# Ranking the experts of a mixture on chip, with 32 token places for 44 of them

## The reference

```python
s = jax.nn.sigmoid((t @ router_w).astype(jnp.float32))
choice = s + router_bias.astype(jnp.float32)
...
_, eidx = lax.top_k(jnp.where(emask, choice, -jnp.inf), TOP_K)
...
gates = jnp.sum(jax.nn.one_hot(eidx, N_EXPERTS, dtype=jnp.float32) * w[..., None], axis=1)

def expert_step(acc, p):
    wg, wu, wd, g = p
    hid = jax.nn.silu(t @ wg) * (t @ wu)
    return acc + (hid @ wd) * g[:, None].astype(t.dtype), None

routed, _ = lax.scan(expert_step, jnp.zeros_like(t), (exp_w_gate, exp_w_up, exp_w_down, gates.T))
shared = (jax.nn.silu(t @ sh_w_gate) * (t @ sh_w_up)) @ sh_w_down
return (routed + shared).reshape(bsz, seq, d)
```

## Time and profile before

| | us |
|---|---|
| median of three runs | 1352.79 |
| lowest and highest of them | 1348.95, 1353.19 |
| the profiled execution | 1356.98 |
| its span, from the first to the last instruction | 1355.2 |
| TensorE busy in it | 1303.0 |
| VectorE busy | 484.7 |
| ScalarE busy | 324.2 |
| GpSimd busy | 77.8 |

### The profile page before, as it was taken

How to read it: one execution, slowest core, us unless ns; L and a number is a source line. 1 busy time by engine, 2 the same in 40 slices (tenths; PEclk the granted TensorE clock), 3 DMA queues, 4 the chain that set the end, 5 groups by cost and what they waited for, 6 DMA issues and landing times.

```text
span 1355.2 us, 17876 instructions
## 1 busy us (share of the span) xinstructions
PE 1303.0 (96%) x6452; PEld 711.2 (52%) x6452; DVE 484.7 (36%) x1079; ACT 324.2 (24%) x789; POOL 77.8 (6%) x100
## 2 busy tenths in 40 slices
PE   7988999999999999999799999999999999999995
PEld 4764744454444444544488857445544444445442
DVE  2583623333222333332432326333332223333324
ACT  3562212222121222221123222122121122221211
POOL 1352100000000000000150000000000000000000
PEclk8988899999999999999899999999999999999998
DMA  8162459999999999999861234599999999999991
GB/s 336 59 249 93 179 206 415 418 418 416 418 411 415 420 419 418 418 416 415 284 213 63 91 126 186 221 416 417 420 418 416 410 418 418 418 418 416 417 416 59
DMA packets 75730, 447.29 MB, mean 330 GB/s; under 512 B 7452, under 2 KB 20184, under 8 KB 25511
## 3 DMA queue, kind: packets, MB, share of 16 engines
q1 hardware_dynamic: 72640, 439.25, 79.6%
q0 software_dynamic: 1904, 6.46, 1.3%
q10 hardware_dynamic: 1142, 1.01, 0.2%
HBM read 445.61 MB, written 1.05 MB: 330 GB/s over the span
## 4 chain that ended last, share of the span: by engine, by line
PE 92%; DVE 2%; issue 2%; DMA 2%; ACT 1%; ACTq 0%; POOL 0%; DVEq 0%; POOLq 0%
PE bank L933 33%; PE bank L955 17%; PE bank L907 10%; PE bank L1001 9%; PE bank L757 4%; PE bank L793 4%; PE bank L861 2%; PE bank L670 2%; PE bank L943 2%; PE bank L796 2%; DMA mixT<-in_l_conv_w 1%; PE bank L970 1%; PE bank L899 1%; PE bank L630 1%; DVE side L1340 1%
## 5 line engine op out<-in xcount | busy, mean ns | idle before, releaser
L933 PE MATMUL bank<-ring,big 128*64 128x512 f32 x2048 | 446.5, 594 | 0.2 <-issue 0.2
L933 PEld LDWEIGHTS bank<-ring,big 128*64 128x64 f32 x2048 | 146.0, 137 | 278.0 <-issue 278.0
L955 PE MATMUL bank<-ring,big 128*64 128x512 f32 x1024 | 233.9, 599 | 2.2 <-ACT big L1213 2.2
L1609 DVE SCALAR_TENSOR_TENSOR ys_low<-bank,gcol,ys_high 128x512 fp32r<-128x512 f32 x128 | 96.1, 751 | 204.1 <-ACT ys_high L1219 204.1
L1601 DVE TENSOR_TENSOR big<-big,bank 128x256 f32<-128x256 f32 x64 | 27.0, 422 | 373.6 <-ACT big L1209 373.6
L907 PE MATMUL bank<-pick,xs_high 128*128 128x256 f32 x512 | 136.3, 302 | 0.0
L1219 ACT ACTIVATE ys_high<-bank,gcol 128x512 fp32r<-128x512 f32 x128 | 88.0, 688 | 192.0 <-PE bank L955 192.0
L955 PEld LDWEIGHTS bank<-ring,big 128*64 128x64 f32 x1024 | 67.8, 136 | 120.6 <-issue 109.7
L907 PE MATMUL bank<-pick,xs_low 128*128 128x256 f32 x512 | 126.5, 282 | 0.0
L1209 ACT ACTIVATE big<-bank 128x256 f32<-128x256 f32 x64 | 24.5, 383 | 405.8 <-PE bank L933 405.8
L907 PEld LDWEIGHTS bank<-pick,xs_high 128*128 128x128 f32 x512 | 97.6, 191 | 26.0 <-issue 24.8
(11 more groups left out here) (236 smaller groups left out, 1108.6 us busy)
## 6 DMA issues: line engine op xcount, KB each, us to landing
ring<-in_l_exp_w_gate SPq DMA_DIRECT2D x128, 1024.0 KB, 9.3
ring<-in_l_exp_w_up SPq DMA_DIRECT2D x128, 1024.0 KB, 11.4
ring<-in_l_exp_w_down SPq DMA_DIRECT2D x128, 1024.0 KB, 15.3
ring<-in_l_w_in SPq DMA_DIRECT2D x12, 1024.0 KB, 12.3
ring<-in_l_w_out SPq DMA_DIRECT2D x8, 1024.0 KB, 6.0
ring<-in_l_w_in SPq DMA_DIRECT2D x4, 1440.0 KB, 15.8
par<-in_l_ln_g POOLq DMA_DIRECT2D x4, 512.0 KB, 7.0
par<-in_l_ln_b POOLq DMA_DIRECT2D x4, 512.0 KB, 7.8
```

Source lines behind the costliest of these rows:

```text
L933: ins = mm(ps[SLOTS * q:SLOTS * q + SLOTS, :], xg[:, c, SLOTS * j:SLOTS * j + SLOTS], both[:, c], start=(c == 0), stop=(c == C - 1))
L955: ins = mm(ps[SLOTS * q:SLOTS * q + SLOTS, :], hidT[pr][:, m, SLOTS * q:SLOTS * q + SLOTS], wt[:, m, HALF * h:HALF * h + HALF], start=(m = ...
L1609: ins = v.scalar_tensor_tensor(ys[1][:, pr, part], ps[:], gcol[:, pr:pr + 1], ys[0][:, pr, part], ALU.mult, ALU.subtract)
```

## The change

The experts are ranked by their number of tokens, on chip. Experts 0 to 7 (`NATURAL`) keep ranks 0 to 7; the other 56 follow by falling count. Ranks 0 to 19 (`NWIDE`) are worked on as before, in five groups of 64 places: one "first", three "wide" and one "turn" (`KINDS`). The other 44 experts get 32 places (`NSLOT`), in eleven "narrow" groups of four. A further round runs if an expert has more tokens than the places of its rank.

The ranking takes place in the first group. VectorE compares the counts (`ranks`) and makes a permutation `perm`; TensorE flips `routed` (the old `posm` and `gates` in one tile) and multiplies it by `perm` (`sort`); VectorE reads the tables back in the new order, with the expert numbers by rank in `order` (`ordered`). SyncE loads the four expert numbers of a group from `order` ahead of its refill. Five small GpSimd operations prepare constants for it.

A narrow group runs in three stages of four weight units each: the gates of four experts in four column tiles of 32 places, then their ups, then their downs. Its gathers have 128 columns instead of 256 and go two chunks to a bank (`pairs`), and its scatter has 8 matmuls instead of 16. SyncE refills its units by kind: four gates, four ups, four downs (`BY_KIND`).

```diff
+NSLOT = 32
+NATURAL = 8
+KINDS = (("first", 1), ("wide", 3), ("turn", 1), ("narrow", 11))
+BEGIN = {"first": 0, "wide": 1, "turn": 4, "narrow": 5}
+NWIDE = GE * BEGIN["narrow"]
...
-        u.loop(L, seq, NGRP, but=("gather",))
+        narrow = [("gT", 0), ("gate", 0), ("up", 1), ("hT", 1)] + [(("dn", h), 2 + h) for h in range(2)] + pair
+        narrow += [(("scatter", n), 6 + n % 2) for n in range(4)]
+        times = dict(KINDS)
+        u.loop((L, "first"), wide + [("rowsT", 6), ("sorted", 7)] + gather + scatter, times["first"])
+        u.loop((L, "wide"), wide + gather + scatter, times["wide"])
+        u.loop((L, "turn"), wide + pair + scatter, times["turn"])
+        u.loop((L, "narrow"), narrow, times["narrow"], but=("pair",))
...
+    if kind == "narrow":
+        return ("gate", "up", ("dn", 1))[w]
     return ("gu", j // 2) if w < 2 else ("dn", j // 2, 1)
...
+BY_KIND = [(j, w) for w in range(3) for j in range(GE)]
...
+                def refill(lp, experts):
+
+                    for j, w in BY_KIND if lp.kind == "narrow" else IN_ORDER:
+                        lp.read(sp, last_use_of_weights(lp.kind, j, w))
+                        sp.dma_start(loop_weights(L, j, w), expert_weights(L, experts[j], w))\
+                          .then_inc(S(f"unit_full{loop_unit(L, j, w)[0]}"), 16)
+
+                def in_place(at):
+
+                    return [sp.value_load(order[0:1, bass.ds(at + j, 1)], min_val=0, max_val=NE - 1) for j in range(GE)]
+
+                refill(ExpertLoop(L, "first", banks, S, bank, i=0), [GE + j for j in range(GE)])
+                sp.wait_ge(S("order"), L + 1)
...
+                lp = ExpertLoop(L, "narrow", banks, S, bank)
+                with sp.Fori(0, dict(KINDS)["narrow"] - 1) as i:
+                    lp.i = i
+                    refill(lp, in_place(lp.groups(GE, GE)))
...
+                def pairs(lp, cs):
+
+                    n = GE * NSLOT
+                    for c in cs:
+                        ps = lp.open(pe, ("pair", c))
+                        for s in range(2):
+                            for tb in range(TB):
+                                for k in range(2):
+                                    ins = mm(ps[:, n * s:n * s + n], xs[k][:, tb, P * (2 * c + s):P * (2 * c + s) + P],
+                                             pick[:, tb, 0:n], start=(tb + k == 0), stop=(tb + k == 2))
+                        lp.made(ins, ("pair", c))
+
+                def sort(lp):
+
+                    lp.moved(pe, "rowsT")
+                    pe.wait_ge(S("perm"), L + 1)
+                    ps = lp.open(pe, "sorted")
+                    for tb in range(TB):
+                        mm(ps[:, P * tb:P * tb + P], routedT[:, tb, :], perm, start=True, stop=True)
+                    mm(ps[0:1, 2 * P:2 * P + NE], expert[0:NE], perm[0:NE, 0:NE], start=True, stop=True)
+                    ins = mm(ps[0:1, 3 * P:3 * P + NE], rank[0:NE, 1:2], perm[0:NE, 0:NE], start=True, stop=True)
+                    lp.made(ins, "sorted")
...
+                    if lp.kind == "first":
+                        ps = lp.open(pe, "rowsT")
+                        for tb in range(TB):
+                            ins = flip(ps[:, P * tb:P * tb + P], routed[:, tb, :, :].rearrange("p a b -> p (a b)"), ident[:])
+                        lp.made(ins, "rowsT")
                     pe.wait_ge(lp.sem("pick"), lp.count(2, 2, 0))
...
+                    for w, key in enumerate(("gate", "up")):
+                        ps = lp.open(pe, key)
+                        for j in range(GE):
+                            weights_landed(lp, j, w)
+                        for c in range(C):
+                            for j in range(GE):
+                                r = slice(NSLOT * j, NSLOT * j + NSLOT)
+                                ins = mm(ps[r, 0:HID], xn[:, c, r], loop_weights(L, j, w)[:, c, :],
+                                         start=(c == 0), stop=(c == C - 1))
+                        lp.made(ins, key)
+
+                    if not last:
+                        pe.wait_ge(lp.sem("pick"), lp.count(2, 2, 1))
+                        pairs(lp, (0, 1))
...
+                    lp.moved(pe, "hT")
+                    for j in range(GE):
+                        weights_landed(lp, j, 2)
+                    for h in range(2):
+                        ps = lp.open(pe, ("dn", h))
+                        for m in range(2):
+                            for j in range(GE):
+                                r = slice(NSLOT * j, NSLOT * j + NSLOT)
+                                ins = mm(ps[r, :], hidT[0][:, m, r], loop_weights(L, j, 2)[:, m, HALF * h:HALF * h + HALF],
+                                         start=(m == 0), stop=(m == 1))
+                        lp.made(ins, ("dn", h))
...
-                v.memset(gates[:], 0.0)
-                v.memset(posm[:], FAR)
...
+                def ranks():
+
+                    v.memset(perm, 0.0)
+                    link(v.tensor_tensor_reduce(where_key.rearrange("p (a e) -> p a e", a=2),
...
+                    link(v.tensor_scalar(over_cap, rank_key, rank[:, 1:2], None, ALU.is_gt))
+                    link(v.tensor_reduce(rank[:, 0:1], over_cap, AX.X, ALU.add))
+                    for half_of in range(2):
+                        at = slice(NE * half_of, NE * half_of + NE)
+                        ins = v.tensor_scalar(perm[at, at], iota[at, :], rank[at, 0:1], None, ALU.is_equal)
+                    ins.then_inc(S("perm"), 1)
+
+                def ordered(lp):
+
+                    ps = lp.read(dve, "sorted")
...
+                    v.tensor_copy(in_turn[:, :, :, 0:NE], ps[:, 0:TB * P].rearrange("p (a k e) -> p a k e", a=TB, k=2))
+                    v.tensor_copy(order[0:1, :], ps[0:1, 2 * P:2 * P + NE]).then_inc(S("order"), 1)
```

More of the change, by code:

```diff
@@ L282, in run_groups, with last_use_of_weights @@
             group(lp)
[L283 to L289 removed]
+    lp.u = 0
+def last_use_of_weights(kind, j, w):
+    if kind == "narrow":
+        return ("gate", "up", ("dn", 1))[w]
     return ("gu", j // 2) if w < 2 else ("dn", j // 2, 1)
@@ L1008, in prog_tensor @@
                 pe.wait_ge(S("xs"), 2 * L + 2)
-                pe.wait_ge(lp.sem("pick"), 1)
+                pe.wait_ge(S(f"moe{L}_pick"), 1)
                 for c in range(C):
                     bank_made(gather(c, bank_open(pe, ("gather", L, c))), ("gather", L, c))
-                run_groups(pe, lp, group)
+                wide(ExpertLoop(L, "first", banks, S, bank, i=0))
+                for i in range(dict(KINDS)["wide"]):
+                    wide(ExpertLoop(L, "wide", banks, S, bank, i=i))
@@ L1237, in prog_scalar @@
                 for c in range(0, C, 2):
                     gathered(bank_read, bank_done, ("gather", L, c))
-                lp = ExpertLoop(L, banks, S, bank)
-                run_groups(act, lp, group)
+                wide(ExpertLoop(L, "first", banks, S, bank, i=0))
+                for i in range(dict(KINDS)["wide"]):
+                    wide(ExpertLoop(L, "wide", banks, S, bank, i=i))
+                wide(ExpertLoop(L, "turn", banks, S, bank, i=0))
+                lp = ExpertLoop(L, "narrow", banks, S, bank)
@@ L1594, in group, with wide @@
+                def wide(lp):
+                    after = "narrow" if lp.kind == "turn" else "wide"
+                    if lp.kind == "first":
+                        ranks()
                     lp.read(dve, "gT")
-                    if not last:
-                        select(lp, lp.groups(GE, GE), lp.count(2, 2, 1))
+                    select(lp, after, lp.groups(GE, GE), lp.count(2, 2, 1))
                     def hidden(pr):
                         ps = lp.read(dve, ("gu", pr))
-                        dve.wait_ge(lp.sem("silu"), lp.count(GE // 2, 0, pr + 1))
+                        dve.wait_ge(lp.own("silu"), lp.own_count(GE // 2, pr + 1))
```

359 lines of the change are left out of this document (248 added, 111 removed).

## The result

The changed kernel takes 1343.79 us (median of nine runs, 1340.85 to 1349.16) beside 1353.18 for the kernel before: the ratio is 0.9932, with a 95% interval of 0.9914 to 0.995. It is faster by 9 us, where 22 were forecast: inside the forecast's range, near its upper end, and with less than half of the gain. The profiled execution has a span of 1345.2 us, 10.0 less than before.

The account below looks back on a forecast made before the run. TensorE was taken to bound the kernel at 30.20 us a group, DMA just behind at 29.8. Per layer 14.3 - 2.5 - 1.0 = 10.8, for two layers 21.6, took 1352.8 to 1331 us; range 1320 to 1347.

Parts of the forecast that it names:

- (e): Way from layer 0 to layer 1: input weights queue behind the last downs but land before TensorE reads them; cost 0.
- the lead: End of a layer: TensorE still works 14.5 us after the last weight byte, landed 8.7 us after group 15 began.
- (a): Eleven narrow groups in four column tiles: DMA sets 29.8 us a group, gaining 14.3 us a layer (10.5 to 17.8).
- (b): First group of each layer ranks the experts: longer bank wait, flips and sort cost 2.5 us (1.2 to 4).
- (c): SyncE's loads of four expert numbers ahead of each refill, 2.4 us a group, covered by queued transfers: cost 0.
- (d): GpSimd's five small operations fall where it is idle, work taken from VectorE lies beside shared expert's matmuls: cost 0.
- (f): TensorE's clock falls in pauses ahead of the ups; only a layer's last downs are on the path: cost 1.0 us.
- No dip between stages: Rival of no change: queue runs dry between narrow groups' stages, 30.9 us a group, 1351 us in all; chance 9%.
- no clock that stays low over whole groups: Rival of a slower kernel: TensorE at 1.2 GHz throughout, 33.4 us a narrow group, 1429 us in all; chance 8%.
- no further round: Rival: experts with too many tokens add 16 groups, 483 us a layer, over 1800; 3% together with anything unseen.
- four tiles and not two: Narrow groups: if only two tiles overlap, TensorE ends 3.5 us a layer later, 1338 us, inside the forecast's range.

## Why the prediction was wrong, point by point

The mechanism was right and three terms of the sum were not: the way to layer 1 (e), put at 0, cost 4.9 us; the lead in (a), read at 8.7 us, was 10.1 to 11.4; and the first group (b), put at 2.5 a layer, cost 3.8 to 4.0.

**What bounds the kernel: right.** The stream sets the narrow groups, 29.83 us and 422 GB/s without a dip (forecast 29.8 and 422), and half the bytes bring TensorE's own 19.6 (forecast 19.4). Gates 3.66 us and downs 3.64 for 3.5 where the clock is up, so four tiles do overlap; the pause ahead of the ups 6.37 for 6.4. The Trainium skill's bad case (TensorE: Matmul & The Clock Gate, section Loop structure matters more than you think) came as the prediction weighed it: the clock falls in every group's pause from the second narrow group on, and its mean is 0.83 to 0.90 over a group. The group takes 29.83 us all the same, since it has 10 us of slack. The loads of the order, (c), and GpSimd's part, (d), cost nothing that shows.

**The end of a layer, (a) and (f): 2.7 to 3.2 us a layer too good.** From group 5's first gates to the end of the last downs the forecast has 310.9 + 1.0, the profile 315.1 and 314.6. In layer 1 the last unit has landed at 1322.6, 309.05 us after those gates, where the sum has 8.7 + 298.2 = 306.9. The ten groups behind group 5 took 298.4 and 299.0 us, as forecast; what failed is the lead, since group 5's last unit landed 11.4 and 10.1 us after its first gates and not 8.7. The 8.7 was misread from the kernel before. The prediction took the us from 1323 for the last with weights in it, but two more follow:

```profile
1324.00:1325.00 1.00, 1.00 (x8) 0.38 (x6) 0.00 (x0) 0.00 (x0) 0.00 (x0) 1.00 0.08 33
1325.00:1326.00 1.00, 1.00 (x8) 0.34 (x6) 0.00 (x0) 0.00 (x0) 0.00 (x0) 1.00 0.06 25
```

Group 15's last unit landed there at 1326.5, 11.8 us after the group began, and group 5's 9.9 and 9.7 us after. TensorE thus worked 11.3 us after the last unit and not 14.5, and so much less was to be gained. The last downs, mostly at half clock, take 5.0 to 5.4 us: of the doubling (3.6 us) 1.4 to 1.7 came, where 1.0 was taken. The sum of all this lies within the ends that the prediction had kept; the lead had no bounds of its own.

**The first group, (b): 3.8 and 4.0 us for 2.5.** The wait was there, at 1.2 us, and the flips and the sort at 1.1 to 1.6. The step that failed is the end of the sum: a pause that grows from 1.1 to 2.3 us also takes the clock away from the work behind it, 1.0 to 1.7 us. The prediction knew that mechanism and looked for it only in the narrow groups, where slack covers it, and not at the one place where it had itself lengthened a pause on the path. Moving the flips and adding the wait to the kernel before both show it.

**The way to layer 1, (e): 4.9 us for 0.** This is the largest miss at any one place. The prediction asked whether the input weights are late (they are not) and left out that TensorE's next instructions must be there too. Behind the experts it goes on at a place whose code isn't loaded; the next load comes 6 us later while the engines carry weights; and in the changed program that next load lies ahead of the projection, where in the program before the projection is under way when it comes. The profile of before had the sign, the 1.53 us of "issue" with no releaser ahead of the flips at 671.02, and the prediction passed over it.

The rest, some 0.5 us a layer, lies in the turn to narrow groups, whose first gates begin that much later; its cause is open. Summed: 2 x (1.4 + 2.9 + 0.5) + 4.9 = 14.5 us of the forecast's 21.6 are lost, and 2.9 came by the other stretches, the start above all, which the change isn't shown to explain: 10.0 in the profile.

**The rivals.** No dip between stages, no clock that stays low over whole groups, no further round, four tiles and not two. What took the gain was not among them. That the range held the time is in part luck: its end of 1347 came from bounds of (a), (b) and (f), not from a term for a stop at a seam.

## What to carry to other kernels

When a change ends a loop's bound by TensorE, cost the places where the loop is entered and left as carefully as the loop: here the loop's period was what was forecast, and its two ends and the way between the layers took more than half of the gain back. Read when the last byte lands from the time at which its transfer is reported landed, and not from a rate that has begun to fall. A wait on the path is priced with the clock of the work behind it, and a jump out of a loop with a load of code, which came at half the pace beside a full DMA queue here; look for "issue" in the chain of waits, move small work out of the pause, and keep the queue clear for the few us in which an engine continues elsewhere. Three such edits brought 14 us, more than the change itself.

## What the runs showed of the hardware that was not expected

- Code is loaded while the kernel runs, in packets of 16 KB through the same DMA engines as the weights, and TensorE stood still for it, 2.60 and 3.56 us between the layers. Two loads in a row came 6 to 6.5 us apart beside weights at 350 GB/s and 3 us apart beside idle engines; in the run with 32 more matmuls two came 0.5 us apart.
- TensorE's clock stayed up over a pause of 1.1 us and fell over one of 2.3 to 2.6 us, in layer 0 and in layer 1, with the ranking and without; the work behind it took 1.0 to 1.7 us longer.
- Four column tiles of 32 overlapped almost in full: the 32 records of the downs took 3.6 us, 0.45 for four, where one tile alone starts a record every 0.43 us.
